# A hybrid decoder layer on one core: two token blocks of the attention branch are split in the second mixer, the first branch pair takes its high terms first, GpSimd's order is rewritten, and one sum of w_out moves later

## The reference

```python
h = rms_norm(x, norm_w)
proj = h @ w_in + b_in                      # all heads, gates and values
attn = sliding_window_sink_attention(a_q, a_k, a_v, sinks)
branch_a = (attn * silu(a_z)) @ w_branch_attn
mq, mk = split(silu(causal_conv(concat(m_q, m_k))))
h_m = head_rms_norm(mlstm_chunkwise(mq, mk, m_v, m_i, m_f), mlstm_norm_w)
branch_m = (sigmoid(m_o) * h_m * silu(m_z)) @ w_branch_mlstm
merged = sigmoid(g_attn) * branch_a + sigmoid(g_mlstm) * branch_m
out = rms_norm(x + merged @ w_out, final_norm_w)
```

## Time and profile before

| | us |
|---|---|
| median of the three runs | 1074.06 |
| the profiled execution | 1072.99 |
| its span | 1071.3 |
| PE busy / DVE / POOL / ACT in the span | 1053.1 / 774.6 / 687.8 / 539.8 |
| DMA moved | 131.79 MB |

### The profile page before, as it was taken

How to read it: one execution, slowest core, us unless ns; L and a number is a source line. 1 busy time by engine, 2 the same in 40 slices (tenths; PEclk the granted TensorE clock), 3 DMA queues, 4 the chain that set the end, 5 groups by cost and what they waited for, 6 DMA issues and landing times.

```text
span 1071.3 us, 18681 instructions
## 1 busy us (share of the span) xinstructions
PE 1053.1 (98%) x6343; PEld 853.0 (80%) x6343; DVE 774.6 (72%) x1186; ACT 539.8 (50%) x1286; POOL 687.8 (64%) x469
## 2 busy tenths in 40 slices
PE   7999999999999999999999999999999899999997
PEld 6887887877877888888878888888777788788886
DVE  5964785776866967776776686769588647766897
ACT  7544755746646643554445454545466345113543
POOL 3577555556555569668966797569859984635441
PEclk9999999999999999999999999999999999999999
DMA  6225132132151232224313433232329439676424
GB/s 221 71 93 90 41 119 80 41 119 74 44 158 49 80 118 80 83 56 137 119 51 92 126 92 94 88 117 89 102 94 376 137 118 330 205 275 260 166 99 137
DMA packets 122078, 131.79 MB, mean 123 GB/s; under 512 B 7884, under 2 KB 97288, under 8 KB 120472
## 3 DMA queue, kind: packets, MB, share of 16 engines
q1 hardware_dynamic: 107048, 84.42, 25.7%
q10 hardware_dynamic: 14960, 46.47, 12.7%
HBM read 96.16 MB, written 34.70 MB: 122 GB/s over the span
## 4 chain that ended last, share of the span: by engine, by line
PE 88%; POOL 3%; DVE 2%; DMA 2%; ACT 1%; DVEq 1%; POOLq 1%; issue 0%; ACTq 0%; SPq 0%
PE ps L1104 66%; PE ps L1407 5%; PE ps L1011 4%; PE ps L1221 3%; POOL ring_lo L836 2%; PE ps L1202 2%; PE ps L1276 2%; PE ps L1348 1%; POOL t L831 1%; PE ps L1330 1%; PE ps L1345 1%; DVE u_m L2704 1%; PE ps L1342 1%; PE ps L1296 1%; PE ps L1363 1%; DMA ev<-gm_scratch 1%
## 5 line engine op out<-in xcount | busy, mean ns | idle before, releaser
L836 POOL TENSOR_TENSOR ring_lo<-w,ring_hi 128x512 fp32r<-128x512 f32 x144 | 213.3, 1503 | 86.8 <-ACT ring_hi L1539 86.8
L836 POOL TENSOR_TENSOR ring_lo<-t,ring_hi 128x512 fp32r<-128x512 f32 x108 | 152.2, 1414 | 141.3 <-ACT ring_hi L1539 141.3
L1104 PE MATMUL ps<-s_hi,ring_hi 128*128 128x512 f32 x576 | 228.7, 397 | 1.8 <-issue 1.8
L1104 PE MATMUL ps<-s_lo,ring_hi 128*128 128x512 f32 x576 | 225.1, 391 | 0.0
L1104 PE MATMUL ps<-s_hi,ring_lo 128*128 128x512 f32 x576 | 225.0, 391 | 0.0
L1104 PE MATMUL ps<-h_hi,ring_hi 128*128 128x512 f32 x432 | 170.7, 395 | 2.6 <-POOL ring_lo L836 1.4
L1104 PE MATMUL ps<-h_lo,ring_hi 128*128 128x512 f32 x432 | 169.0, 391 | 0.0
L1104 PE MATMUL ps<-h_hi,ring_lo 128*128 128x512 f32 x432 | 168.6, 390 | 0.0
L1539 ACT ACTIVATE ring_hi<-w 128x512 fp32r<-128x512 f32 x144 | 86.7, 623 | 110.4 <-PE ps L1104 93.7
L1104 PEld LDWEIGHTS ps<-s_hi,ring_hi 128*128 128x128 f32 x576 | 108.2, 188 | 26.0 <-issue 5.1
L1104 PEld LDWEIGHTS ps<-s_hi,ring_lo 128*128 128x128 f32 x576 | 108.2, 188 | 22.4
(11 more groups left out here) (317 smaller groups left out, 2072.0 us busy)
## 6 DMA issues: line engine op xcount, KB each, us to landing
w<-in_w_in SPq DMA_DIRECT2D x128, 256.0 KB, 2.9
xs<-in_x SPq DMA_DIRECT2D x8, 512.0 KB, 8.2
ga_scratch<-ev ACTq DMA_DIRECT2D x4, 1024.0 KB, 4.1
u_scratch<-silu_z ACTq DMA_DIRECT2D x8, 512.0 KB, 3.2
c_rows<-c_scratch ACTq DMA_DIRECT2D x8, 512.0 KB, 6.7
ev<-u_scratch SPq DMA_DIRECT2D x8, 512.0 KB, 4.6
u_sums_scratch<-ev ACTq DMA_DIRECT2D x4, 1024.0 KB, 5.0
gm_scratch<-ev ACTq DMA_DIRECT2D x4, 1024.0 KB, 5.1
```

The source lines that it names most:

```text
L836: return nc.gpsimd.tensor_tensor(flat(lo[:]), flat(raw_or_sum[:]), flat(hi[:]).bitcast(F32), ALU.subtract)
L1104: mm = nc.tensor.matmul(ps[:, bank, columns], w[:, k, :], h[:, k, columns], start=(m == 0), stop=(m == PRODUCT - 1))
```

## The change

There are five parts.

1. **Two blocks split in the second mixer.** Besides block 6, block 5 is now split in each mLSTM step. DVE's sums stand a chunk earlier (c == 1), ACT copies the high part at half steps, `branch_sum_low(half)` is called twice, and the one large store becomes five stores. SP loads block 5 as high and low part, 2 x 1024 KB where it was 1024 KB. ACT's `block_high(5)` and DVE's `block_low(5)` are gone.
2. **High terms first.** Pair 32 has its own PE code, `first_branch_pair`: of each product first four matmuls high by high, then a wait for the low weights, four with them, then a wait for the block's low part and four with it.
3. **GpSimd in order of need.** In pair 32 the sum t4 is made after the low parts 2 and 7, and low part 5 stands before 3. In pairs 33 to 35 low parts 1 and 6 are made as soon as their inputs are.
4. **Small moves.** SP loads w21 of pair 33 after w12, and every w21 of the branch pairs waits for all sums of the pair before. ACT's first loads of gate rows (`gate_row`), which wait for a store, move behind the high parts of pair 33. `block_low(1)` is made one product earlier.
5. **w_out.** The sum `f_s2` moves from n == 1 to n == 2.

```diff
+        US_FIRST, US_ALL = 48, 80
             def branch_weights(a):
+                def lower_left():
+                    sp.wait_ge(sum_made, 4 * n)
+                    sp.wait_ge(w2_ready, n)
+                    sp.dma_start(w21[:], wba_cols[:, KH:KT, first]).then_inc(w21_in, 16)
...
-                if n == 6:
-                    sp.dma_start(s4[0][:].bitcast(F32), scr_uh.rearrange("k p n -> p k n")).then_inc(u_in[n], 16)
-                    into = s4[1][:].bitcast(F32)
+                if n >= 5:
+                    high, into = BLOCKS[n][0][:].bitcast(F32), BLOCKS[n][1][:].bitcast(F32)
+                    sp.dma_start(high, scr_uh[6 - n].rearrange("k p n -> p k n")).then_inc(u_in[n], 16)
                 sp.dma_start(into, src.rearrange("k p n -> p k n")).then_inc(u_in[n], 16)
...
+            def first_branch_pair(i):
+                first_sum(i)
+                second_sum(i)
+                third_sum()
+                low_1(i)
+                low_6(i)
+                low_2(i)
+                low_7(i)
+                fourth_sum(i)
+                low_4(i)
+                low_5(i)
+                low_3(i)
+
+            def branch_pair(i):
+                first_sum(i)
+                low_1(i)
+                second_sum(i)
+                low_6(i)
+                third_sum()
+                fourth_sum(i)
+                lows_of_pair(i)
...
+                def in_parts(n, ring_slot, w_low):
+                    hi, lo = BLOCKS[n]
+                    if n < 5:
+                        pe.wait_ge(u_hi, n + 1)
+                    else:
+                        pe.wait_ge(u_in[n], 32)
+                    part(product_bank(n, None), ring_slot[0], hi, first=True)
+                    pe.wait_ge(w_low, i + 1)
+                    part(product_bank(n, None), ring_slot[1], hi)
+                    if n < 5:
+                        pe.wait_ge(u_split, n + 1)
+                    return part(product_bank(n, None), ring_slot[0], lo, last=True)
...
+                split_4, store_4, split_1, store_1 = ((4, 1), (5, 1), (7, 0), (8, 0)) if last else \
+                    ((1, 1), (2, 1), (3, 1), (4, 1))
+                def branch_step(step):
+                    if step == split_4:
+                        act.wait_ge(us_made, 3 * p + 1)
+                        act.sem_inc(passed, 1)
+                        A(us_hi[:], ev[:, 1, token_half(0)], ACT.Copy).then_inc(s_hi, 1)
+                    if step == store_4:
+                        act.wait_ge(us_made, 3 * p + 2)
...
+                    if step == split_1:
+                        act.wait_ge(us_out, US_ALL * p + US_FIRST)
+                        act.sem_inc(passed, 1)
+                        A(us_hi[:], ev[:, 1, token_half(1)], ACT.Copy).then_inc(s_hi, 1)
...
-                    if a == 0 and q == 0:
-                        block_high(5)
-                    if q == 3 and not last:
+                    if q == (3 if a else 5) and not last:
...
-                        for n in {2: (0,), 5: (1,), 6: (2, 3)}.get(q, ()):
+                        for n in {2: (0,), 4: (1,), 6: (2, 3)}.get(q, ()):
...
-                    if c == 2 and not last:
+                    if c == 1 and not last:
                         branch_sums()
-                    if c == (5 if last else 3):
-                        branch_sum_low()
+                    if c == (5 if last else 2):
+                        branch_sum_low(0)
+                    if c == 4 and not last:
+                        branch_sum_low(1)
...
                             block_low(4)
-                            block_low(5)
...
                     V.tensor_tensor(f_s3[:], f_o11[:], f_o21[:], ALU.subtract).then_inc(wo_sum, 1)
-                    dve.drain()
+                if n == 2:
                     V.tensor_tensor(f_s2[:], f_s1[:], f_o11[:], ALU.subtract)
```

173 lines of the change are left out of this document (112 added, 61 removed).

## The result

The changed kernel takes 1076.13 us (median of 22 runs, 1074.42 to 1079.11), the kernel before 1074.0 us in the same rounds. The ratio is 1.0021 with a 95% interval of 1.0014 to 1.0029, so +2.3 us, where -2.6 (1071.5) was predicted. It lies inside the 0.3% that the prediction counts as no change, but on the other side and outside the range. The profiled executions say the same: 1075.48 against 1072.99 us. Runs of one kernel spread by more than 4 us: of 35 later ones of the kernel before, 19 took 1072.15 to 1072.94 us and 16 took 1074.20 to 1076.56.

A forecast was written before the change was run, and what follows sets the result against it. PE was taken as the bound, losing 5.95 + 1.12 = 7.1 us in pauses. Terms -1.0 (pairs), -1.1 (w_out), 0 (steps) gave -2.1: 1070.9 from the profiled run, 1072.0 from the timed median, middle 1071.5; range 1067.8 to 1074.3.

The forecast's parts named there:

- The steps: mLSTM steps: the added DVE, ACT and DMA work fits beside dense matmuls, 0 us; bounds 0 and +2.6 per step.
- The tight place: Steps 0 to 2, c == 1: four sums precede the accumulator's release; 3.7 us, release 1.1 us early, so 0.
- turns: DVE (two SBUF inputs) and POOL exclude each other and alternate; each such 128x2048 DVE instruction costs POOL 2.1 us.
- The stall rival: mLSTM steps, release at c == 1: earlier sums stall PE, two more turns per step, +5.7 us, 1077.2; chance 10%.
- The last step: Last mLSTM step: ACT's tanh and chunk 6 come 1.3 us late, just covered; 0, at most +1 us.
- Pair 32: First branch pair: pauses before products 2, 7 and 5 go, 2.7 us won by product 3's end; pair's net -1.0.
- The pause at product 4: Pair 32: product 4's low part waits for DVE's block 4, then POOL; a new loss of 1.3 us inside it.
- Transfers: Branch pairs: one more 1024 KB load costs 2.7 us; DMA stays at its rate until some 832 us.
- First sum of pair 33: POOL, pair 33: starts when w12 lands, about 832.6 us, instead of at 833.23.
- The pause in pair 33: PE, pair 33: product 6 waits 2.5 us for low 6, which stands behind DVE's normalisation; product 2 starts at 845.1.
- w_out: w_branch_mlstm tiles: with the third sum moved, the 1.12 us pause before tile 3 goes, nothing given back: -1.1 us.
- Past product 2 of pair 33 POOL is ahead again: Branch pairs after pair 33's product 2: no pause of PE up to 897 us.

The follow-up runs named there:

- e17: Changed kernel with DVE's denominators made by four instructions with one tensor input instead of two with two; 1.0003, +0.3 us against the kernel before.
- e3: Changed kernel with part 1 (block 5 split in the mLSTM steps) taken back; 1.0003, +0.3 us against the kernel before.
- e14: Kernel before with one more two-input DVE instruction of 128x512 in each of steps 0 to 2, at c == 3; 1.0012, +1.3 us.
- e15: Kernel before with the four sums of steps 0 to 2 at c == 1 instead of c == 2; 1.0002, +0.2 us.
- e4: Changed kernel with pair 32's sum t4 again ahead of low parts 2 and 7 on GpSimd; 1.0026, +2.8 us against the kernel before.
- e8: Changed kernel with 7 more matmuls on PE between products 7 and 4 of pair 32; 1.0019, +2.0 us against the kernel before.
- e1: Kernel before with only w_out's third sum moved from tile 1 to tile 2 (part 5); 0.9986, -1.5 us.
- e9: Changed kernel with GpSimd's order of pairs 34 and 35 as before the change; 1.0005, +0.5 us against the kernel before.

## Why the prediction was wrong

- **The steps: here the prediction failed.** "The tight place is step 0 to 2, c == 1 ... I take 0." The sums' length and the release were right. But turns were priced only at the four sums; the small instructions behind them stand in no term of the sum, which puts them at nothing without a reason. They pay up to 1.3 us each when they meet POOL, in chunks 1 to 3 and 6, and in chunk 6 that hung on 0.12 us; the late chain then makes the normalisation pay 0.94 us as well, and the 1.14 us of room before the turning do not cover it. Missed: +3.25 us. The stall rival (10%) had a price per step of 1.3 to 2.6, somewhat above the 0.9 to 1.2 that came, but at the wrong place: its release was in time. Shown by e17 (removes it), e3 (belongs to part 1), e14 and e15 (neither of these two pieces alone does it). The rival's total of 1077.2 is also added up wrongly: +5.7 on 1073.5, the middle of the two times of before that the sum starts from, is 1079.2; 1077.2 takes the 2.1 off twice.
- **The last step, 0 to +1.** PE waits 0.34 us for chunk 7's input (`k_w`) in the profile after, and pair 32 starts 0.31 us later against the turning. Inside the bounds.
- **Pair 32.** Pauses before products 2, 7 and 5 gone: right; 0.50 us inside product 1 came in their place. The pause at product 4 was given as 1.3 us inside it; it is 1.7 in front of it, since the order of turns was the other one: DVE first, then low part 2. That the sum t4 was moved back and would be waited for was right; that it should be moved forward again does not follow (e4).
- **Transfers.** DMA at its rate until 832 us: right, in times shifted by the 3.5 us that pair 32 starts later (368 GB/s still in 834:836); "387 to 406 GB/s until 830" was read from two windows, in 824:828 of the kernel before it was 344. First sum of pair 33 at 836.22, in the shifted times 832.7 where 832.6 was predicted. The pause in pair 33 came before product 2, not 6: the turn with the normalisation fell behind low part 6.
- **The clock, not in the prediction (it has no term for it).** 1.62 us lost behind the pause at product 4, about 1.0 of which pair 33 would have waited for anyway (e8). From product 6 of pair 32 to product 2 of pair 33 it is 27.31 us against 27.75: -0.4 where -0.9 was predicted.
- **w_out.** "Nothing is given back" held for w_out itself (e1: -1.25 in its stretch). "Past product 2 of pair 33 POOL is ahead again" was the wrong sentence: pair 35's low part 1 in the new order cost 0.86 us at tile 0 (e9).
- **Sum.** -2.1 predicted; steps +3.25, last step and pairs +0.5 instead of -1.0, tiles -0.4 instead of -1.1.
